# Gate and up lines with one matmul of 512 columns for both halves of the activation

## The chip, the cores and the metric

The kernel runs on one core of a Trainium2 chip. The metric is the device time of one execution in microseconds (us). Before the change it is 1159.81 us, the median of 3 runs (1159.59 to 1160.43).

## The reference

The program computes two blocks on 256 tokens (272 with 16 meta tokens) of 1024 features. The first block has two layers with two kinds of attention. The second block has a feed-forward stage, a mixer (gated linear attention and sparse attention), a second feed-forward stage and an embedding stage. The change concerns the two feed-forward stages, called ffn0 and ffn1 in the kernel:

```python
def swiglu(x, w_in, w_out):                      # w_in 1024 x 5632, w_out 2816 x 1024
    gate, up = jnp.split(x @ w_in, 2, axis=-1)
    return (jax.nn.silu(gate) * up) @ w_out

h = h + 0.5 * swiglu(rms_norm_2(h, ffn1_norm[i]), ffn1_w_in[i], ffn1_w_out[i])
h = h + hybrid_mixer(...)
h = h + 0.5 * swiglu(rms_norm_2(h, ffn2_norm[i]), ffn2_w_in[i], ffn2_w_out[i])
```

All is float32. The factor of the norm is the same for all features of a token, so the kernel multiplies by it after the matmuls (`scale`).

## The kernel before

Features lie on the 128 partitions and tokens along the free dimension. A float32 value is split in two parts of the shorter type float32r: a rounded high half (`_hi`) and the rest (`_lo`). A product of two such values is summed from three matmuls: high weight by high activation, high weight by low activation, low weight by high activation.

**Lines and units.** A "line" is 128 output features of one projection: 8 k-tiles of 128 inputs ("down" in the feed-forward stages: 11), three matmuls each, all into one bank of PSUM. A "unit" holds the weights of two lines (16 blocks of 128 x 128, 1 MB). Of the feed-forward stages, unit j for j = 0 to 21 is gate line j and up line j, and 16 units of 11 blocks follow for the two halves of each of 8 down lines.

**Where the weights come from.** SP loads unit u into one of three slots of `raw` (`load_unit`, L726) once the low halves of unit u-3 have been made. ACT rounds the unit to `w_hi` in two instructions (`cut_to`, L866; L875 and L876), once PE has finished the lines of unit u-3. DVE subtracts, `w_lo = raw - w_hi`, in four pieces of 512 columns (L1343; four of 384, 384, 384 and 256 in a down unit). For some lines elsewhere POOL does this; never in a feed-forward stage. `lo_after` (L1348) fixes in which place of DVE's program the pieces come: behind gate line j the last two pieces of unit j+1, behind up line j the first two of unit j+2. PE waits for the pieces that a line needs before its first matmul.

**A turn of a feed-forward stage.** Each engine has one queue and works in the order of its program. All five programs are written out by hand; the sequence for each j is this.

- PE: gate line j, then up line j (`line`, L2128; its matmuls have line 2147). The lines use four banks in turn (`line0`, `line1`, `result0`, `result1`), and a line waits until the line four places before has been read out.
- DVE: gate line j times `scale` into `prod` (L1415), `act_lo` of j-1 (L1758), two pieces of w_lo, in ffn0 for j = 2 to 9 one `first_result` (L1739), up line j times `scale` into `prod2` (L1415), two pieces of w_lo, and the two instructions of `finish` (L1750: (tanh + 1) times gate; L1753: times up). Turn 1 of ffn0 also has the two instructions of `last_norm`.
- ACT: the two `w_hi` instructions of unit j+2, tanh of gate line j (L1112), `act_hi` of j-1 (L1103).

`act_lo` of j-1 waits for `act_hi` of j-1, and ACT makes that only after tanh of j, which waits for gate line j.

Ahead of ffn0 and ffn1 the factor of the norm is computed by PE, ACT and DVE in turn (`root_of`, `rstd_of`); meanwhile PE already runs the first lines. Behind the turns come 16 half down lines; DVE adds each to `h`.

Of the kernel before, what the change touches and what calls it, by code (L numbers as in the profile page):

```python
# [54 lines left out]
SH = 8  # L55
# [435 lines left out]
class Alloc:  # L491
# [11 lines left out]
    def sem(self, name):  # L503
        return self.stack.enter_context(self.nc.semaphore(name))
# [5 lines left out]
def hybrid_blocks_kernel(nc, weights, tokens, embeds, small_in, small2_in, rpb, consts_in, consts2_in, levels_in,  # L510
# [7 lines left out]
    w_lo = sb("w_lo", [CUT, UB * P], F32R)  # L518

    h = sb("h", [KT, TOK])  # L520
    x_hi = sb("x_hi", [KT, TOK], F32R)
    x_lo = sb("x_lo", [KT, TOK], F32R)
    y_hi = sb("y_hi", [KT, TOK], F32R)
    y_lo = sb("y_lo", [KT, TOK], F32R)
    wide = sb("wide", [KT, TOK])
    scale = sb("scale", [TOK])
    root = sb("root", [2, TOK])
# [88 lines left out]
    od_hi_ready, od_ready = sem("od_hi_ready"), sem("od_ready")  # L616
    p_hi_ready, p_ready, pp_ready = sem("p_hi_ready"), sem("p_ready"), sem("pp_ready")
    pg_raw, pg_used = sem("pg_raw"), sem("pg_used")
    means_ready = sem("means_ready")
    gate_ready = sem("gate_ready")  # L620
    stored = sem("stored")
    hg_ready, last_root, out_pool = sem("hg_ready"), sem("last_root"), sem("out_pool")

    first, second = (x_hi, x_lo), (y_hi, y_lo)
    x_of = dict(layer0=first, mixed0=first, layer1=second, mixed1=second, ffn0=first, mixer=first, mixed2=first,
                ffn1=second, embed=first)
    y_of = dict(layer0=second, layer1=first)
# [44 lines left out]
    mean_p = a2.sb("mean_p", [P])  # L672
    levels = a2.sb("levels", [len(HALVES) + 1, P], U32)
    p_in = turned[:, :, 0:SEQ]
    p_hi = a2.sb("p_hi", [2, SEQ], F32R)
    p_lo = a2.sb("p_lo", [2, SEQ], F32R)
    pp = wide[:, :, 0:SEQ]
    a3 = Alloc(nc)
    act_hi = a3.sb("act_hi", [FT, SEQ], F32R)
    act_lo = a3.sb("act_lo", [FT, SEQ], F32R)  # L680
    a3.close()
    a3 = Alloc(nc)
    gg_hi, gg_lo = y_hi[:, :, 0:SEQ], y_lo[:, :, 0:SEQ]
    low = turned[:, 0, 0:SEQ]
    index_k = a3.sb("index_k", [SEQ])
    index_q = a3.sb("index_q", [PAIRS, SEQ])
# [16 lines left out]
    a4 = Alloc(nc)  # L703
    dq = wide[:, :, 0:SEQ]
    mgate = {n: a4.sb(f"mgate_{n}", [KT, SEQ]) for n in "gs"}
    od_hi = a4.sb("od_hi", [SH, SEQ], F32R)
    od_lo = a4.sb("od_lo", [SH, SEQ], F32R)

    rbias = a4.sb("rbias", [RING, SEQ])
    score = root[:, :, 0:SEQ]  # L710
# [151 lines left out]
    def _(act):  # L862
# [235 lines left out]
        def ffn(f):  # L1098
            name = f"ffn{f}"

            def round_act(j):
                act.wait_ge(act_full, FT * f + j + 1)
                act.activation(act_hi[:, j], prod2[:, j % 2, 0:SEQ], ACT.Copy).then_inc(act_hi_ready, 1)  # L1103

            for j in range(FT):
                cut_to(UNIT[(name, "gate", j)] + CUT - 1)
                n = FT * f + j
                act.wait_ge(act_raw, n + 1)

                if j >= 2:  # L1110
                    act.wait_ge(act_half, n - 1)
                act.activation(th[:, j % 2, 0:SEQ], prod[:, j % 2, 0:SEQ], ACT.Tanh, scale=0.5).then_inc(act_tanh, 1)  # L1112
                if j:
                    round_act(j - 1)
            round_act(FT - 1)
# [162 lines left out]
        cut_to(STAGES["ffn1"] + CUT - 1)  # L1278
        root_of(("ffn1", "norm"), SEQ)
        act.wait_ge(embeds_in, 16)  # L1280
        act.activation(p_hi[:, :, :], p_in, ACT.Copy).then_inc(p_hi_ready, 1)
        ffn(1)


# [34 lines left out]
    def _(dve):  # L1319
# [423 lines left out]
        def ffn(f):  # L1743
            name = f"ffn{f}"

            def finish(j):

                n = FT * f + j
                dve.wait_ge(act_tanh, n + 1)
                dve.scalar_tensor_tensor(prod[:, j % 2, 0:SEQ], th[:, j % 2, 0:SEQ], 1.0, prod[:, j % 2, 0:SEQ],  # L1750
                                         ALU.add, ALU.mult).then_inc(act_half, 1)
                dve.wait_ge(act_half, n + 1)
                dve.tensor_tensor(prod2[:, j % 2, 0:SEQ], prod[:, j % 2, 0:SEQ], prod2[:, j % 2, 0:SEQ],  # L1753
                                  ALU.mult).then_inc(act_full, 1)

            def rest_of_act(j):
                dve.wait_ge(act_hi_ready, FT * f + j + 1)
                dve.tensor_tensor(act_lo[:, j], prod2[:, j % 2, 0:SEQ], act_hi[:, j].bitcast(F32),  # L1758
                                  ALU.subtract).then_inc(act_ready, 1)

            for j in range(FT):
                scaled_line((name, "gate", j), prod[:, j % 2, 0:SEQ]).then_inc(act_raw, 1)
                if j:
                    rest_of_act(j - 1)
                lo_after(name, "gate", j)
                if f == 0 and j == 1:
                    last_norm()
                if f == 0 and 2 <= j < KT + 2:
                    first_result(j - 2)
                scaled_line((name, "up", j), prod2[:, j % 2, 0:SEQ]).then_inc(act_up, 1)  # L1770
                lo_after(name, "up", j)
                dve.wait_ge(act_up, FT * f + j + 1)
                finish(j)
            rest_of_act(FT - 1)
            for m in range(KT):

                dve.scalar_tensor_tensor(h[:, m, 0:SEQ], line_wait((name, "down", m, 0))[:, 0:SEQ], 0.25,
                                         h[:, m, 0:SEQ], ALU.mult, ALU.add).then_inc(down_used, 1)
                lo_after(name, "down", m, 0)
                if m:  # L1780
                    rest_of_h(("mixer", "embed")[f], m - 1, SEQ)
                dve.wait_ge(down_used, KT * f + m + 1)
                dve.scalar_tensor_tensor(h[:, m, 0:SEQ], line_wait((name, "down", m, 1))[:, 0:SEQ], 0.25,
                                         h[:, m, 0:SEQ], ALU.mult, ALU.add).then_inc(h_ready, 1)
                if m < KT - 1:
                    lo_after(name, "down", m, 1)
            one_piece()
            dve.wait_ge(h_ready, H_BATCH[name] + KT)
            rest_of_h(("mixer", "embed")[f], KT - 1, SEQ)
            lo_after(name, "down", KT - 1, 1)  # L1790
# [289 lines left out]
        lo_after("mixer", "mix", KT - 1)  # L2080
        rstd_of(("ffn1", "norm"), SEQ, scale[:, 0:SEQ])
        dve.wait_ge(p_hi_ready, 1)
        dve.tensor_tensor(p_lo[:, :, :], p_in, p_hi[:, :, :].bitcast(F32), ALU.subtract).then_inc(p_ready, 1)
        ffn(1)


# [28 lines left out]
    def _(pe):  # L2115
# [15 lines left out]
        def line(key, n, src=None, depth=KT, first=0, at=None, ready=None, last=None):  # L2131


            if at is None:
                at = key[-1] % 2 * KT
            hi, lo = unit(key)
            src_hi, src_lo = src or x_of[key[0]]
            bank = line_open(key)
            for k in range(depth):
                if last and k == depth - 1:  # L2140
                    last()
                if ready:
# [252 lines left out]
        def ffn(f):  # L2395
            name = f"ffn{f}"
            for j in range(FT):
                if j == 0:
                    line((name, "gate", j), SEQ, at=0, ready=x_tile(name), last=(lambda: norm_sum(name, SEQ)) if f else None)
                else:  # L2400
                    line((name, "gate", j), SEQ, at=0)
                line((name, "up", j), SEQ, at=KT)
                if (f, j) == (0, 0):

                    two_norm_sums()
            for m in range(KT):
                for half in range(2):
                    first = half * FT // 2
                    line((name, "down", m, half), SEQ, (act_hi, act_lo), FT // 2, first, 0,
                         ready=(lambda k: pe.wait_ge(act_ready, FT * f + first + k + 1)) if m == 0 else None)  # L2410

        ffn(0)
# [38 lines left out]
        def line_by_token(key):  # L2451
# [1 line left out]

            t = key[2] % TILES
            hi, lo = (w.rearrange("p (m k) c -> p k m c", m=2) for w in unit(key))
            src_hi, src_lo = (x[:, :, t * P:(t + 1) * P] for x in x_of[key[0]])
            bank = line_open(key)[:, 0:2 * P].rearrange("p (m c) -> p m c", c=P)
            for k in range(KT):
                for m, (stay, move) in enumerate([(src_hi, hi), (src_hi, lo), (src_lo, hi)]):
# [103 lines left out]
        for i in range(len(DSA_JOBS) + 2):  # L2563
            if i < len(DSA_JOBS):
# [1 line left out]
                if i == KT:  # L2566
                    pe.wait_ge(gg_ready, KT)
                name, m = DSA_FILLERS[i]
                line(("mixer", name, m), SEQ, (gg_hi, gg_lo) if name == "yg" else None)
            if 1 <= i <= len(DSA_JOBS):  # L2570
                dsa_turn(i - 1)
            if i >= 2:
                dsa_values(i - 2)
        for m in range(KT):
            line(("mixer", "ys", m), SEQ, (od_hi, od_lo),
                 ready=(lambda k: pe.wait_ge(od_ready, k + 1)) if m == 0 else None)
        for m in range(KT):
            line(("mixer", "mix", m), SEQ, x_of["mixed2"], ready=x_tile("mixed2") if m == 0 else None)
# [1 line left out]
        ffn(1)  # L2580
        pe.wait_ge(p_ready, 1)
        for m in range(KT):
            line(("embed", "pp", m), SEQ, (p_hi, p_lo), 2, 0, 2 * m)
        for m in range(KT):
            if m == 0:
                line(("embed", "pg", m), SEQ, ready=x_tile("embed"), last=lambda: norm_sum("embed", SEQ))
# [157 lines left out]
```

## Time and profile before

| | |
|---|---|
| median of 3 runs | 1159.81 us |
| span of the profiled execution | 1158.5 us |
| PE busy | 1118.8 us (97%) |
| DVE busy | 826.3 us (71%) |
| ACT busy | 628.0 us (54%) |
| POOL busy | 256.3 us (22%) |
| chain that ended last | PE 79%, DVE 13%, ACT 4% |
| granted clock of PE over the span | 0.9 to 1.0 of full in each of 40 slices |

The page and the views come from one profiled execution. Its own time is not listed beside the runs; its span, from the first to the last instruction on the engines, is 1158.5 us, and the median of the runs lies 1.3 us above it. Matmuls are pipelined: the profile gives one of 256 columns 0.28 us, but in a full stream the next starts 0.12 us later. So the time of a stretch of matmuls is read from their starts, and busy time on PE means only that the stream did not stop. Instructions of DVE and ACT overlap by 0.08 us in the same way where the second does not wait for the first.

### The profile page before, as it was taken

To read this page: it belongs to the slowest core of one execution; us is meant where nothing else is said; L and a number is where in the kernel's file an instruction comes from. 1 tells how busy PE (TensorE), PEld (TensorE's weight loads), DVE (VectorE), ACT (ScalarE), POOL (GpSimd) and SP (SyncE) were. 2 spreads that over 40 slices of the span, in tenths; PEclk is the share of its full clock that TensorE was granted. 3 is DMA by queue.
4 is the path that set the end of the run, shared out by engine and by line. 5 is a ranking of instruction groups with operands and counts; after the bars stand their busy time and mean duration, and the time that the engine had idled before them with its cause. 6 is when DMAs were issued, how large, how long until landed. Compare 5 with 4: busy or idle time off the path is not lost.

```text
span 1158.5 us, 23093 instructions
## 1 busy us (share of the span) xinstructions
PE 1118.8 (97%) x9108; PEld 1096.5 (95%) x9108; DVE 826.3 (71%) x1843; ACT 628.0 (54%) x1164; POOL 256.3 (22%) x214
## 2 busy tenths in 40 slices
PE   6999999999999999999999999989999999999996
PEld 6999999999999999999999999978999999999995
DVE  7964356879544687888766799577857877777666
ACT  6555545564655547544444653584455654444464
POOL 1056553200656614000000008300770000000000
PEclk9999999999999999999999999999999999999998
DMA  6454333354433434555455453225453555544551
GB/s 244 154 182 146 110 120 105 128 178 154 184 132 124 154 116 167 216 189 184 163 194 190 180 203 127 110 76 173 175 168 139 191 182 182 182 171 176 180 203 37
DMA packets 38635, 185.05 MB, mean 160 GB/s; under 512 B 12536, under 2 KB 14840, under 8 KB 19968
## 3 DMA queue, kind: packets, MB, share of 16 engines
q1 hardware_dynamic: 38528, 183.57, 45.2%
q8 instruction: 73, 1.20, 0.4%
q14 instruction: 34, 0.28, 0.1%
HBM read 182.49 MB, written 1.06 MB: 158 GB/s over the span
## 4 chain that ended last, share of the span: by engine, by line
PE 79%; DVE 13%; ACT 4%; issue 2%; DMA 1%; DVEq 0%; POOL 0%; SPq 0%; ACTq 0%
PE line L2147 49%; PE result L2147 18%; DVE w_lo L1343 4%; PE line L2460 2%; PE turn L2304 1%; PE result L2338 1%; PE score L2281 1%; PE score L2479 1%; PE stat L2338 1%; PE score L2285 1%; ACT w_hi L876 1%; ACT w_hi L875 1%; DVE root L1378 1%; DVE rstd L1365 1%; PE score L2147 1%
## 5 line engine op out<-in xcount | busy, mean ns | idle before, releaser
L852 POOL TENSOR_TENSOR w_lo<-raw,w_hi 128x512 fp32r<-128x512 f32 x168 | 224.2, 1366 | 545.7 <-ACT w_hi L875 545.6
L1343 DVE TENSOR_TENSOR w_lo<-raw,w_hi 128x512 fp32r<-128x512 f32 (+2 forms) x544 | 338.2, 666 | 3.0 <-ACT w_hi L910 2.0
L2147 PE MATMUL line<-x_hi,w_hi 128*128 128x256 f32 (+1 forms) x1048 | 309.1, 295 | 16.0 <-DVE x_lo L1399 9.3
L2147 PE MATMUL line<-x_hi,w_lo 128*128 128x256 f32 (+1 forms) x1048 | 299.1, 285 | 0.0
L2147 PE MATMUL line<-x_lo,w_hi 128*128 128x256 f32 (+1 forms) x1048 | 298.8, 285 | 0.0
L875 ACT ACTIVATE w_hi<-raw 128x1024 fp32r<-128x1024 f32 (+1 forms) x177 | 179.5, 1014 | 91.1 <-PE line L2147 36.5
L2147 PEld LDWEIGHTS line<-x_hi,w_hi 128*128 128x128 f32 x1048 | 199.4, 190 | 22.7 <-issue 13.5
L2147 PEld LDWEIGHTS line<-x_lo,w_hi 128*128 128x128 f32 x1048 | 199.1, 190 | 0.9
L2147 PEld LDWEIGHTS line<-x_hi,w_lo 128*128 128x128 f32 x1048 | 199.6, 190 | 0.0
L2147 PE MATMUL line<-y_hi,w_hi 128*128 128x256 f32 (+1 forms) x656 | 192.6, 294 | 1.0 <-DVE y_lo L1407 0.3
L2147 PE MATMUL line<-y_hi,w_lo 128*128 128x256 f32 (+1 forms) x656 | 185.4, 283 | 0.0
L2147 PE MATMUL line<-y_lo,w_hi 128*128 128x256 f32 (+1 forms) x656 | 185.2, 282 | 0.0
L876 ACT ACTIVATE w_hi<-raw 128x1024 fp32r<-128x1024 f32 (+1 forms) x178 | 175.6, 987 | 0.0
L2147 PEld LDWEIGHTS line<-y_hi,w_hi 128*128 128x128 f32 x656 | 123.8, 189 | 2.9 <-DVE w_lo L1343 0.9
L2147 PEld LDWEIGHTS line<-y_lo,w_hi 128*128 128x128 f32 x656 | 123.5, 188 | 0.8
L2147 PEld LDWEIGHTS line<-y_hi,w_lo 128*128 128x128 f32 x656 | 124.0, 189 | 0.0
L2147 PE MATMUL result<-x_hi,w_hi 128*128 128x256 f32 (+1 forms) x232 | 65.8, 283 | 0.1
L2147 PE MATMUL result<-x_lo,w_hi 128*128 128x256 f32 (+1 forms) x232 | 65.4, 282 | 0.0
L2147 PE MATMUL result<-x_hi,w_lo 128*128 128x256 f32 (+1 forms) x232 | 65.4, 282 | 0.0
L858 POOL TENSOR_TENSOR wide<-hg,rstd 128x512 f32<-128x512 f32 x1 | 1.7, 1702 | 285.2 <-DVE rstd L1365 285.2
L1017 ACT ACTIVATE probs<-score,top 128x272 f32<-128x272 f32 (+2 forms) x66 | 29.6, 449 | 57.4 <-DVE top L1563 35.4
L2147 PE MATMUL result<-y_lo,w_hi 128*128 128x256 f32 x192 | 54.1, 282 | 0.0
(376 smaller groups left out, 2354.0 us busy)
## 6 DMA issues: line engine op xcount, KB each, us to landing
raw<-in_weights SPq DMA_DIRECT2D x145, 1024.0 KB, 4.8
raw<-in_weights SPq DMA_DIRECT2D x32, 704.0 KB, 4.1
rel_raw<-in_rpb SPq DMA_DIRECT2D x64, 24.0 KB, 4.8
h<-in_tokens SPq DMA_DIRECT2D x2, 544.0 KB, 6.4
raw<-in_weights SPq DMA_DIRECT2D x2, 512.0 KB, 6.3
rbias<-bias_by_distance SPq DMA_DIRECT2D x8, 128.0 KB, 4.9
out<-wide SPq DMA_DIRECT2D x4, 256.0 KB, 2.5
consts<-in_consts SPq DMA_DIRECT2D x1, 960.0 KB, 7.1
```

What stands on the lines that cost most here:

```text
L852: pool.tensor_tensor(w_lo[:, u % CUT, at], raw[:, u % RAW, at], w_hi[:, u % CUT, at].bitcast(F32), ALU.subtract).then_inc(lo_pool, 1)
L875: act.activation(w_hi[:, v % CUT, 0:half], raw[:, v % RAW, 0:half], ACT.Copy).then_inc(hi_cut, 1)
L876: act.activation(w_hi[:, v % CUT, half:n], raw[:, v % RAW, half:n], ACT.Copy).then_inc(hi_cut, 1)
L1017: act.activation(probs[0:m, place % 2, first:first + keys], score_bank[s % 2][0:m, 0:keys], ACT.Exp, bias=top[0:m, n % 2, 0:1], scale=-1.0 ...
L1343: dve.tensor_tensor(w_lo[:, u % CUT, at], raw[:, u % RAW, at], w_hi[:, u % CUT, at].bitcast(F32), ALU.subtract).then_inc(lo_cut, 1)
L1365: ins = dve.scalar_tensor_tensor(r if out_ is None else out_, v, -3.0, r, ALU.add, ALU.mult)
L1378: dve.scalar_tensor_tensor(v, stat_at(key)[:, 0:n], EPS, v, ALU.add, ALU.mult).then_inc(stat_read, 1)
L2147: ins = pe.matmul(bank[:, 0:n], stay, move[:, first + k, 0:n], start=(k, m) == (0, 0), stop=(k, m) == (depth - 1, 2))
L2281: ins = pe.matmul(s[:, 0:TOK], qa[:, c, t * P:(t + 1) * P], ka_half[:, half * TOK:(half + 1) * TOK], start=True, stop=True)
L2285: ins = pe.matmul(s[:, 0:KEYS_B], qb[:, c, t * P:(t + 1) * P], kb[:, c, t, half], start=True, stop=True)
L2338: ins = pe.matmul(single_bank[pair % 2][:, cols], tn[:, b * P:(b + 1) * P], v[:, kt, cols], start=(half, b) == (0, 0), stop=b == both)
L2460: ins = pe.matmul(bank, stay[:, k], move[:, k], start=(k, m) == (0, 0), stop=(k, m) == (KT - 1, 2))
```

## The change

In gate and up lines the two matmuls that share the high half of a weight become one. It moves both halves of the activation past it, 512 columns in two separate runs of 256, and fills the bank: columns 0 to 255 get high by high, columns 256 to 511 high by low. The third matmul (low weight by high activation) adds to columns 0 to 255 as before. To make the two halves reachable by one operand they now lie in one buffer (`x`, `y`, and for the sake of one helper also `act`, `p`, `od`).

The two column ranges must now be added. ACT copies the upper one to SBUF (`low_sum`), DVE adds the lower one (`both_sums`), waits for its own result and multiplies by `scale`. There is one place for each copy (gate, up), so a copy waits until the copy before has been used.

```diff
+TWO_SUMS = {_g for _g in LINES if _g[1] in ("gate", "up")}
...
-    x_hi = sb("x_hi", [KT, TOK], F32R)
-    x_lo = sb("x_lo", [KT, TOK], F32R)
+    x = sb("x", [2, KT, TOK], F32R)
...
+    low_sums, sums_of_line = wide[:, 0:2, 0:SEQ], wide[:, 2:4, 0:SEQ]
...
# ACT
+            def low_sum(kind, j):
+
+                at = int(kind == "up")
+                bank = line_wait((name, kind, j))
+                if FT * f + j:
+                    act.wait_ge((act_raw, act_up)[at], FT * f + j)
+                act.activation(low_sums[:, at], bank[:, SEQ:2 * SEQ], ACT.Copy).then_inc(low_sum_out, 1)
+
             for j in range(FT):
-                cut_to(UNIT[(name, "gate", j)] + CUT - 1)
+                low_sum("gate", j)
                 n = FT * f + j
                 act.wait_ge(act_raw, n + 1)
...
                 act.activation(th[:, j % 2, 0:SEQ], prod[:, j % 2, 0:SEQ], ACT.Tanh, scale=0.5).then_inc(act_tanh, 1)
+                low_sum("up", j)
                 if j:
                     round_act(j - 1)
...
# DVE
+            def both_sums(kind, j, dst):
+                at = int(kind == "up")
+                bank = line_wait((name, kind, j))
+                dve.wait_ge(low_sum_out, 2 * (FT * f + j) + at + 1)
+                link(dve.tensor_tensor(sums_of_line[:, at], bank[:, 0:SEQ], low_sums[:, at], ALU.add))
+                return dve.tensor_tensor(dst, sums_of_line[:, at], scale[:, 0:SEQ], ALU.mult)
...
-                scaled_line((name, "gate", j), prod[:, j % 2, 0:SEQ]).then_inc(act_raw, 1)
+                both_sums("gate", j, prod[:, j % 2, 0:SEQ]).then_inc(act_raw, 1)
...
-                scaled_line((name, "up", j), prod2[:, j % 2, 0:SEQ]).then_inc(act_up, 1)
+                both_sums("up", j, prod2[:, j % 2, 0:SEQ]).then_inc(act_up, 1)
...
# PE
+                if key in TWO_SUMS:
+
+                    pe.matmul(bank[:, 0:2 * n].rearrange("p (h t) -> p h t", h=2), hi[:, at + k], both[:, :, first + k, 0:n],
+                              start=k == 0, stop=False)
+                    ins = pe.matmul(bank[:, 0:n], lo[:, at + k], src_hi[:, first + k, 0:n], start=False,
+                                    stop=k == depth - 1)
+                    continue
```

(`line_wait` on ACT begins with `cut_to`, so the `w_hi` instructions keep their place.)

DVE in a turn of ffn1 before the change (`prod` is both `prod` and `prod2`), from the gate line to the next:

```order
L1415 TENSOR_TENSOR prod<-line,scale 128x256 [waits line_done]
L1758 TENSOR_TENSOR act_lo<-prod,act_hi 128x256 [waits act_hi_ready]
L1343 TENSOR_TENSOR w_lo<-raw,w_hi 128x512 [waits hi_cut] x2
L1415 TENSOR_TENSOR prod<-line,scale 128x256 [waits line_done]
L1343 TENSOR_TENSOR w_lo<-raw,w_hi 128x512 [waits hi_cut] x2
L1750 SCALAR_TENSOR_TENSOR prod<-th,prod 128x256 [waits act_tanh,act_up]
L1753 TENSOR_TENSOR prod<-prod 128x256 [waits act_half]
L1415 TENSOR_TENSOR prod<-result,scale 128x256 [waits line_done]
```

The same turn on DVE after the change (`wide` holds the copied and the added sums, `act` is both halves of the activation):

```order
L1769 TENSOR_TENSOR wide<-line,wide 128x256 [waits low_sum_out,line_done]
L1770 TENSOR_TENSOR prod<-wide,scale 128x256 [waits dve_step]
L1784 TENSOR_TENSOR act<-prod,act 128x256 [waits act_hi_ready]
L1362 TENSOR_TENSOR w_lo<-raw,w_hi 128x512 [waits hi_cut] x2
L1769 TENSOR_TENSOR wide<-line,wide 128x256 [waits low_sum_out,line_done]
L1770 TENSOR_TENSOR prod<-wide,scale 128x256 [waits dve_step]
L1362 TENSOR_TENSOR w_lo<-raw,w_hi 128x512 [waits hi_cut] x2
L1776 SCALAR_TENSOR_TENSOR prod<-th,prod 128x256 [waits act_tanh,act_up]
L1779 TENSOR_TENSOR prod<-prod 128x256 [waits act_half]
```

Each scaled line has become two instructions, the first with a wait for ACT and the second with a wait for the first; nothing else has moved.

ACT in the same place before the change, from tanh to tanh:

```order
L1112 ACTIVATE th<-prod 128x256 [waits act_raw]
L1103 ACTIVATE act_hi<-prod 128x256 [waits act_full]
L875 ACTIVATE w_hi<-raw 128x1024 [waits line_done,raw_in1]
L876 ACTIVATE w_hi<-raw 128x1024
L1112 ACTIVATE th<-prod 128x256 [waits act_half,act_raw]
```

And after the change:

```order
L1130 ACTIVATE th<-prod 128x256 [waits act_raw]
L1121 ACTIVATE wide<-line 128x256 [waits act_up,line_done]
L1113 ACTIVATE act<-prod 128x256 [waits act_full]
L885 ACTIVATE w_hi<-raw 128x1024 [waits line_done,raw_in1]
L886 ACTIVATE w_hi<-raw 128x1024
L1121 ACTIVATE wide<-result 128x256 [waits act_raw,line_done]
L1130 ACTIVATE th<-prod 128x256 [waits act_half,act_raw]
```

The copy of the up line stands between tanh and the rounded activation of the turn before; the copy of the next gate line stands behind the two `w_hi` instructions.

## Rows read from the trace of the kernel before

**Rows 1.** The page: its first line, and the engines' busy time.
```profile
span 1158.5 us, 23093 instructions
PE 1118.8 (97%) x9108; PEld 1096.5 (95%) x9108; DVE 826.3 (71%) x1843; ACT 628.0 (54%) x1164; POOL 256.3 (22%) x214
```

**Rows 2.** Chain of waits, whole span: start us, us, engine and line, matmuls.
```profile
126.17 3.02 PE line L2147 x24
...
577.40 5.68 PE result L2147 x48
...
678.33 5.66 PE line L2460 x48
...
1053.61 7.80 PE result L2147 x66
```

**Rows 3.** Chain of waits, 440 to 482 us.
```profile
476.39 1.30 DVE w_lo L1343 x2
...
477.74 3.11 PE result L2147 x24
```

**Rows 4.** Timeline of DVE in ffn0: start us, us, instruction, idle before.
```profile
502.25 0.42 DVE L1415 TENSOR_TENSOR prod<-result,scale 128x256 f32<-128x256 f32 x1
503.46 0.43 DVE L1758 TENSOR_TENSOR act_lo<-prod,act_hi 128x256 fp32r<-128x256 f32 x1 [0.79 <-ACT act_hi L1103]
503.80 1.29 DVE L1343 TENSOR_TENSOR w_lo<-raw,w_hi 128x512 fp32r<-128x512 f32 x2
505.00 0.48 DVE L1739 SCALAR_TENSOR_TENSOR h<-h,small,rstd 128x256 f32<-128x256 f32 x1
505.40 0.41 DVE L1415 TENSOR_TENSOR prod<-result,scale 128x256 f32<-128x256 f32 x1
505.73 1.28 DVE L1343 TENSOR_TENSOR w_lo<-raw,w_hi 128x512 fp32r<-128x512 f32 x2
506.94 0.42 DVE L1750 SCALAR_TENSOR_TENSOR prod<-th,prod 128x256 f32<-128x256 f32 x1
507.39 0.43 DVE L1753 TENSOR_TENSOR prod<-prod 128x256 f32<-128x256 f32 x1
507.73 0.42 DVE L1415 TENSOR_TENSOR prod<-line,scale 128x256 f32<-128x256 f32 x1
```

**Rows 5.** Timeline of ACT in the same turn.
```profile
502.70 0.42 ACT L1112 ACTIVATE th<-prod 128x256 f32<-128x256 f32 x1 [1.70 <-DVE prod L1415]
503.02 0.40 ACT L1103 ACTIVATE act_hi<-prod 128x256 fp32r<-128x256 f32 x1
504.52 1.06 ACT L875 ACTIVATE w_hi<-raw 128x1024 fp32r<-128x1024 f32 x1 [1.10 <-DMA raw<-in_weights]
```

**Rows 6.** Timeline of DVE at the first and behind the last turn of ffn1.
```profile
933.65 0.69 DVE L2083 TENSOR_TENSOR p_lo<-turned,p_hi 128x512 fp32r<-128x512 f32 x1
934.26 0.42 DVE L1415 TENSOR_TENSOR prod<-result,scale 128x256 f32<-128x256 f32 x1
...
1050.85 0.42 DVE L1415 TENSOR_TENSOR prod<-line,scale 128x256 f32<-128x256 f32 x1
...
1058.12 1.83 DVE L1343 TENSOR_TENSOR w_lo<-raw,w_hi 128x384 fp32r<-128x384 f32 x4
```

**Rows 7.** Timeline of DVE in the first two turns of ffn0.
```profile
465.80 0.76 DVE L1415 TENSOR_TENSOR prod<-line,scale 128x256 f32<-128x256 f32 x2
...
468.46 0.42 DVE L1415 TENSOR_TENSOR prod<-result,scale 128x256 f32<-128x256 f32 x1
...
470.05 0.43 DVE L1758 TENSOR_TENSOR act_lo<-prod,act_hi 128x256 fp32r<-128x256 f32 x1 [1.17 <-ACT act_hi L1103]
...
474.84 0.42 DVE L1415 TENSOR_TENSOR prod<-line,scale 128x256 f32<-128x256 f32 x1
```

**Rows 8.** Timeline of ACT there: the load of the table for tanh.
```profile
465.79 1.28 ACT L1112 ACT_TABLE_LOAD   x1
```

**Rows 9.** Stretches: busy us and count of each engine, PE clock, DMA, GB/s.
```profile
765.00:780.00 15.00, 10.38 (x81) 9.82 (x80) 11.39 (x27) 12.70 (x24) 0.00 (x0) 0.96 0.20 71
...
815.00:830.00 15.00, 13.53 (x111) 13.14 (x110) 14.11 (x45) 6.08 (x11) 10.10 (x8) 1.00 0.57 211
```

More of the change, by code:

```diff
@@ L618, in hybrid_blocks_kernel @@
     pg_raw, pg_used = sem("pg_raw"), sem("pg_used")
+    low_sum_out = sem("low_sum_out")
     means_ready = sem("means_ready")
@@ L622, in hybrid_blocks_kernel, with halves @@
     hg_ready, last_root, out_pool = sem("hg_ready"), sem("last_root"), sem("out_pool")
-    first, second = (x_hi, x_lo), (y_hi, y_lo)
+    def halves(both):
+        return both[:, 0], both[:, 1], both
+    first, second = halves(x), halves(y)
     x_of = dict(layer0=first, mixed0=first, layer1=second, mixed1=second, ffn0=first, mixer=first, mixed2=first,
@@ L674, in hybrid_blocks_kernel @@
     p_in = turned[:, :, 0:SEQ]
-    p_hi = a2.sb("p_hi", [2, SEQ], F32R)
-    p_lo = a2.sb("p_lo", [2, SEQ], F32R)
+    p = a2.sb("p", [2, 2, SEQ], F32R)
+    p_hi, p_lo = p[:, 0], p[:, 1]
+    low_sums, sums_of_line = wide[:, 0:2, 0:SEQ], wide[:, 2:4, 0:SEQ]
     pp = wide[:, :, 0:SEQ]
     a3 = Alloc(nc)
-    act_hi = a3.sb("act_hi", [FT, SEQ], F32R)
-    act_lo = a3.sb("act_lo", [FT, SEQ], F32R)
+    act_both = a3.sb("act", [2, FT, SEQ], F32R)
+    act_hi, act_lo = act_both[:, 0], act_both[:, 1]
     a3.close()
     a3 = Alloc(nc)
-    gg_hi, gg_lo = y_hi[:, :, 0:SEQ], y_lo[:, :, 0:SEQ]
+    gg = y[:, :, :, 0:SEQ]
+    gg_hi, gg_lo = gg[:, 0], gg[:, 1]
     low = turned[:, 0, 0:SEQ]
@@ L705, in hybrid_blocks_kernel @@
     mgate = {n: a4.sb(f"mgate_{n}", [KT, SEQ]) for n in "gs"}
-    od_hi = a4.sb("od_hi", [SH, SEQ], F32R)
-    od_lo = a4.sb("od_lo", [SH, SEQ], F32R)
+    od = a4.sb("od", [2, SH, SEQ], F32R)
+    od_hi, od_lo = od[:, 0], od[:, 1]
     rbias = a4.sb("rbias", [RING, SEQ])
@@ L1280, in _ @@
         act.wait_ge(embeds_in, 16)
-        act.activation(p_hi[:, :, :], p_in, ACT.Copy).then_inc(p_hi_ready, 1)
+        act.activation(p_hi, p_in, ACT.Copy).then_inc(p_hi_ready, 1)
         ffn(1)
@@ L2082, in _ @@
         dve.wait_ge(p_hi_ready, 1)
-        dve.tensor_tensor(p_lo[:, :, :], p_in, p_hi[:, :, :].bitcast(F32), ALU.subtract).then_inc(p_ready, 1)
+        dve.tensor_tensor(p_lo, p_in, p_hi.bitcast(F32), ALU.subtract).then_inc(p_ready, 1)
         ffn(1)
@@ L2136, in line @@
             hi, lo = unit(key)
-            src_hi, src_lo = src or x_of[key[0]]
+            src_hi, src_lo, both = src or x_of[key[0]]
             bank = line_open(key)
@@ L2408, in ffn @@
                     first = half * FT // 2
-                    line((name, "down", m, half), SEQ, (act_hi, act_lo), FT // 2, first, 0,
+                    line((name, "down", m, half), SEQ, halves(act_both), FT // 2, first, 0,
                          ready=(lambda k: pe.wait_ge(act_ready, FT * f + first + k + 1)) if m == 0 else None)
@@ L2455, in line_by_token @@
             hi, lo = (w.rearrange("p (m k) c -> p k m c", m=2) for w in unit(key))
-            src_hi, src_lo = (x[:, :, t * P:(t + 1) * P] for x in x_of[key[0]])
+            src_hi, src_lo = (x[:, :, t * P:(t + 1) * P] for x in x_of[key[0]][:2])
             bank = line_open(key)[:, 0:2 * P].rearrange("p (m c) -> p m c", c=P)
@@ L2568, in _ @@
                 name, m = DSA_FILLERS[i]
-                line(("mixer", name, m), SEQ, (gg_hi, gg_lo) if name == "yg" else None)
+                line(("mixer", name, m), SEQ, halves(gg) if name == "yg" else None)
             if 1 <= i <= len(DSA_JOBS):
@@ L2574, in _ @@
         for m in range(KT):
-            line(("mixer", "ys", m), SEQ, (od_hi, od_lo),
+            line(("mixer", "ys", m), SEQ, halves(od),
                  ready=(lambda k: pe.wait_ge(od_ready, k + 1)) if m == 0 else None)
@@ L2582, in _ @@
         for m in range(KT):
-            line(("embed", "pp", m), SEQ, (p_hi, p_lo), 2, 0, 2 * m)
+            line(("embed", "pp", m), SEQ, halves(p), 2, 0, 2 * m)
         for m in range(KT):
```

3 lines of the change are left out of this document (1 added, 2 removed).

## The prediction

> **What bounds the kernel now.** I read the page first. PE is busy for 1118.8 of 1158.5 us, DVE for 826.3 [rows 1], so at first sight TensorE sets the time and anything that shortens its stream pays. I then followed the chain of waits through the two feed-forward stages (FFN 0, from 461 us; FFN 1, from 931 us), since only their gate and up lines change. In the steady part the chain is PE alone: a turn j (gate line j and up line j, 48 matmuls) takes 5.68 us, 118.3 ns from one matmul to the next; the last turn of FFN 0 ends at 583.08, the last of FFN 1 at 1053.61 [rows 2]. At the start of FFN 0 the same chain shows something else: up line 3 starts at 477.74, 0.05 us after DVE's w_lo pieces for it end at 477.69 [rows 3]. There DVE was the later one. So I read DVE instruction by instruction in a turn where it is behind.
>
> Call G(j) the start of DVE's first instruction on gate line j. From G = 502.25 to the next, 507.73, is 5.48 us [rows 4]. The steps between starts are: gate scaled, then idle until ACT's act_hi, 1.21; act_lo 0.34; two w_lo pieces 1.20; first_result 0.40; up scaled 0.33; two w_lo pieces 1.21; the two halves of `finish` 0.45 and 0.34. Nowhere in it does DVE wait for PE. The idle 0.79 us is a round trip: gate scaled, ACT's tanh 0.45 later, act_hi 0.32 behind it, act_lo 0.44 behind that [rows 4, 5]. The round thus takes 5.48 with first_result (eight turns, j = 2 to 9 of FFN 0) and 5.08 without. PE needs 5.68. The cover is 0.6 us a turn, and 0.2 in those eight: TensorE and the DVE-ACT round are nearly level.
>
> **The change, part by part.**
>
> *TensorE.* For each of 8 k-tiles of 88 lines, two matmuls of 256 columns become one of 512. No line of the trace streams 512 columns past such a weight. Nearest rows: 256 columns take 118.3 ns start to start, 272 take 3.02/24 = 125.8 [rows 2]. At 2.4 GHz (the granted level) 256 columns stream in 107 ns, so each matmul has some 11.6 ns on top, and merging two saves that once. Bounds: 213 ns (512 columns with nothing on top) and 237 (two present ones, nothing saved). I take 225. A line then takes 8 x (225 + 118.3) = 2.75 us instead of 2.84, a turn 5.49. If TensorE alone set the time, 88 x 8 x 11.6 ns = 8.2 us would go. That the 512 columns come from two places I cost at nothing: the L2460 matmuls move two separate runs of 128 columns and take 5.66/48 = 118 ns [rows 2].
>
> The Trainium skill, "TensorE: Matmul & The Clock Gate", section "Back-to-back issue gap", gives about 131 ns a matmul at 512 columns as sustained in a stream with weight loads. By it a line would take 2.0 us and TensorE would be freed of some 70 us. The 256-column rows at 118 ns, which follow the column count, do not fit so small a step, and no row here has 512 columns; the sum below doesn't use it.
>
> *DVE.* Each scaled line (one instruction out of PSUM, with `scale`) becomes an addition and then a multiplication that waits for it. The nearest dependent pair is `finish`, 0.45 from start to start (506.94 to 507.39), the nearest independent step 0.33 to 0.34 [rows 4]. I take 0.45 for each added instruction, so 0.90 a turn. Bounds 0.33 and 0.48 each, the latter a first_result whole.
>
> *ACT.* A copy of 256 columns is like act_hi: 0.32 a step, 0.40 alone [rows 5]. What matters is where it stands. The copy for up line j stands ahead of act_hi(j-1), and DVE waits for act_hi(j-1) before it writes act_lo, the w_lo pieces of unit j+1 and all behind them; those pieces are what PE's up line j+1 waits for. So the up copy adds 0.32 to the round (bounds 0.30 and 0.42). At the start of a stage, where DVE isn't behind, it even has to wait for PE's up line itself. The gate copy adds nothing while DVE is behind: gate line j+1 is done and ACT through its w_hi pieces about 1.8 us before G(j+1). The weight transfers stay covered too: w_hi waits 1.1 us for one at 504.52 [rows 5], and the slot for the next is given free by the w_lo pieces, one round earlier, with the round now longer.
>
> New round: 5.08 + 0.90 + 0.32 = **6.30 us**, and 6.70 with first_result. It is longer than TensorE's 5.49, so DVE and ACT set every turn. What PE does in 5.49 hides behind it, the saving included; PE waits some 0.8 us a turn, at the up line, for w_lo. The round leaves room for a 512-column matmul of up to 6.30/16 - 118 = 276 ns.
>
> *The sum, FFN 1.* G(0) is 934.26 and stays: the first gate copy fits in while DVE makes p_lo [rows 6]. Turn 0 has no act_lo: 0.45 + 0.34 + 1.24 + 0.45 + 0.34 + 1.20 + 0.45 + 0.34 = 4.8, so G(1) = 939.1. 20 rounds of 6.30, and 0.5 for turn 20, which cuts four pieces of 384 columns instead of two of 512, give G(21) = 1065.6. From G(21) to the end of the w_lo pieces of the third "down" unit is 1050.85 to 1059.95 = 9.1 us now [rows 6] and 1.2 more after: 1075.9. TensorE, which started that unit at 1061.41 (1053.61 + 7.80 [rows 2]), then waits for it: **+14.5 us**. After that "down" gives nothing back: its pace is PE's.
>
> *FFN 0.* Here DVE is the later one from the start. Turn 0: the first gate copy delays the sum by 0.4; the up copy stands behind ACT's 1.28 us table load and the tanh, so the up addition starts near 468.25, and G(1) moves from 468.46 to about 471.0. Turn 1 adds 1.2 less the 0.4 which it already waits for ACT (468.46 to 470.05 is 1.59, not 1.21) [rows 7, 8]. G(2) = 474.84 + 3.4 = 478.2. 8 x 6.70 + 11 x 6.30 + 0.5 = 123.4 gives G(21) = 601.6; 10.3 more is 611.9, against 583.08 + 7.80 = 590.88: **+21.0 us**.
>
> At both stage starts the norm matmul comes 0.1 us earlier: -0.2 together. Sum 35.3 us on a span of 1158.5, so 1193.8. The median of the runs, 1159.81, lies 1.3 above the profiled span, which I add: 1195.1. All else in the diff (halves of one buffer instead of two buffers) issues the same instructions.
>
> **Rivals.**
> - *The forecast:* the DVE-ACT round sets the turn, about 1195 us. For it: a round already at 5.48 with no wait for PE in it. Chance 0.82.
> - *TensorE still sets the turn (faster).* The round would have to stay below 5.49: the 1.22 us would have to fit into 0.4. That could be if the additions fell into DVE's idle 0.79 and 0.42 and the act_hi copy didn't wait for the up copy. Against it: both stand in order in one queue, and the idle is itself part of the round. Price: -8.2 + 1159.8 = 1152. Decides from a round of 5.49 down. Chance 0.04.
> - *Half hidden.* The two added instructions cost 0.33 each and the up copy nothing: round 5.74, so 42 rounds x 0.06 over PE's present 5.68, with 3.2 for the eight first_result turns and about 3 at starts and ends: 1169. Chance 0.05.
> - *The clock falls.* PE would pause for 13% of the time. In 765:780, with PE busy for 10.38 of 15 us, the granted clock fell to 0.96 from 1.00; in 815:830, at 13.53 of 15, it stayed at 1.00 [rows 9]. The expected pauses are like the latter. If a tenth of the gate and up turns (27 us at the new pace) ran at 1.2 GHz, their 4.3 turns of 11 us would cost some 20 us more: 1215. Chance 0.05. The Trainium skill, same page, section "A second HAM failure mode: psum-queue depth-cycling", says that short idles between groups at 512 columns made the clock go back and forth in another kernel; the 815:830 row speaks against it at this share of idle.
> - *The wide matmul costs over 276 ns.* At 300 a line takes 3.35 us, a turn 6.70: 1211. No row excludes it; the two-run matmuls of L2460 make it unlikely. Chance 0.04.
>
> **How the numbers follow.** A measurement of this kernel tells 0.2% (2.3 us) from no change. Slower by more than that: forecast, half hidden, clock and wide matmul, 0.95, less 0.01 for what no case names: 0.94. Faster: 0.04. Same: 0.02. The bounds of the added prices move the round from 6.30 to 6.04 (0.33, 0.33, 0.30) or 6.46 (0.48, 0.48, 0.42): 42 rounds, -11 or +7 us, so 1184 to 1202 for the forecast alone. The clock and wide cases pull the upper end to 1209; the half hidden and the faster case stay outside.
>
> **What would show it.** DVE rounds of 6.30 (6.70 for j = 2 to 9 of FFN 0) at even spacing; act_lo starting about 1.98 after G(j) with ACT in the order tanh, copy, act_hi ahead of it; a PE wait near 0.8 us for w_lo at each up line and none at the "down" lines beyond the first few; the first act_lo wait in each stage longest; a 512-column matmul 225 ns from the next. It would be wrong if DVE waited for PE in mid-stage, if the act_hi copy came before the up copy's wait mattered, or if the PE clock row fell below 10 in these slices.

## The result, and the profile after

The changed kernel takes 1198.1 us (median of 4 runs, 1197.8 to 1198.17) against 1159.7 (4 runs) for the kernel before. The ratio is 1.0333, with a 95% interval of 1.032 to 1.0345: slower, by 38 us. The forecast was 1195, within 1184 to 1209.

The page of the kernel after: its first line, the engines' busy time, and PE's and DVE's rows of 40 slices of the span.

```profile
span 1196.1 us, 22033 instructions
PE 1129.7 (94%) x8404; PEld 1065.4 (89%) x8404; DVE 858.7 (72%) x1931; ACT 651.0 (54%) x1252; POOL 256.2 (21%) x214
...
PE   6999999999999998889999999989999999998996
...
DVE  7954456879336687888866799677757788887666
```

PE has 704 matmuls fewer and is nevertheless busy for longer than in [rows 1]: that number counts a running stream, not work. What tells is its share, 94% after 97%, and the 8s in its row that the row before lacks: three slices in ffn0 (448 to 538 us) and one at the down units of ffn1 (1076 to 1106 us). The chain of waits has moved from PE to DVE. Page part 4 of the kernel after, share of the span by engine:

```profile
PE 58%; DVE 27%; ACT 7%; issue 6%; DMA 2%; DVEq 0%; POOL 0%; ACTq 0%; SPq 0%
```

Before, PE had 79% and DVE 13%. This is DVE's timeline for a turn of ffn0 in the kernel after (columns as in [rows 4], which it answers to):

```profile
504.96 0.41 DVE L1769 TENSOR_TENSOR wide<-line,wide 128x256 f32<-128x256 f32 x1
505.41 0.42 DVE L1770 TENSOR_TENSOR prod<-wide,scale 128x256 f32<-128x256 f32 x1
506.90 0.42 DVE L1784 TENSOR_TENSOR act<-prod,act 128x256 fp32r<-128x256 f32 x1 [1.06 <-ACT act L1113]
507.24 1.29 DVE L1362 TENSOR_TENSOR w_lo<-raw,w_hi 128x512 fp32r<-128x512 f32 x2
508.44 0.48 DVE L1758 SCALAR_TENSOR_TENSOR h<-h,small,rstd 128x256 f32<-128x256 f32 x1
508.84 0.41 DVE L1769 TENSOR_TENSOR wide<-line,wide 128x256 f32<-128x256 f32 x1
509.29 0.42 DVE L1770 TENSOR_TENSOR prod<-wide,scale 128x256 f32<-128x256 f32 x1
509.63 1.28 DVE L1362 TENSOR_TENSOR w_lo<-raw,w_hi 128x512 fp32r<-128x512 f32 x2
510.83 0.41 DVE L1776 SCALAR_TENSOR_TENSOR prod<-th,prod 128x256 f32<-128x256 f32 x1
511.28 0.42 DVE L1779 TENSOR_TENSOR prod<-prod 128x256 f32<-128x256 f32 x1
511.63 0.42 DVE L1769 TENSOR_TENSOR wide<-result,wide 128x256 f32<-128x256 f32 x1
```

From 504.96 to 511.63 is 6.67 us (forecast 6.70, before 5.48). Each addition costs 0.45 (504.96 to 505.41, 508.84 to 509.29), and the idle before act_lo has grown from 0.79 to 1.06. ACT's timeline in the same turn shows by what, and answers to [rows 5]:

```profile
505.87 0.42 ACT L1130 ACTIVATE th<-prod 128x256 f32<-128x256 f32 x1 [2.52 <-DVE prod L1770]
506.19 0.37 ACT L1121 ACTIVATE wide<-line 128x256 f32<-128x256 f32 x1
506.46 0.41 ACT L1113 ACTIVATE act<-prod 128x256 fp32r<-128x256 f32 x1
```

The up line's copy stands between tanh and act_hi for 0.27 us (506.19 to 506.46). ACT waits 2.52 us ahead of tanh and does not limit anything by its amount of work. PE pays: its timeline at an up line of ffn1.

```profile
1002.43 0.28 PE L2174 MATMUL result<-y,w_lo 128*128 128x256 f32 x1
1002.55 0.39 PE L2172 MATMUL result<-y,w_hi 128*128 128x512 f32 x1
1002.78 0.28 PE L2174 MATMUL result<-y,w_lo 128*128 128x256 f32 x1
1003.50 0.51 PE L2172 MATMUL result<-y,w_hi 128*128 128x512 f32 x1 [0.43 <-DVE w_lo L1362]
```

The next matmul starts 0.72 us after the last, not 0.12: 0.60 us lost, to w_lo. The idle of 0.43 in brackets is less, since it counts only from the modelled end of the matmul before. Wide to narrow is 0.23 us here, narrow to wide 0.12. The first wide matmul behind the pause takes 0.34 (1003.50 to 1003.84), 0.11 more, and both together are the 0.7 us by which a turn is longer than TensorE's own.

### The profile page after: what moved, and what is told of

Same layout as the page of the kernel before. It is cut to its first block, busy times and chain, and to the rows that moved or that the text cites. A ratio compares the mean times of both kernels' runs of the same rounds, so it can differ in the third digit from the quotient of the medians.

```text
span 1196.1 us, 22033 instructions
## 1 busy us (share of the span) xinstructions
PE 1129.7 (94%) x8404; PEld 1065.4 (89%) x8404; DVE 858.7 (72%) x1931; ACT 651.0 (54%) x1252; POOL 256.2 (21%) x214
## 3 DMA queue, kind: packets, MB, share of 16 engines
HBM read 182.49 MB, written 1.06 MB: 153 GB/s over the span
## 4 chain that ended last, share of the span: by engine, by line
PE 58%; DVE 27%; ACT 7%; issue 6%; DMA 2%; DVEq 0%; POOL 0%; ACTq 0%; SPq 0%
PE line L2180 37%; DVE w_lo L1362 12%; PE result L2180 7%; DVE wide L1769 2%; PE line L2493 2%; DMA raw<-in_weights 2%; DVE prod L1770 2%; ACT wide L1121 1%; PE turn L2337 1%; DVE prod L1776 1%; ACT act L1113 1%; PE result L2371 1%; PE score L2314 1%; PE score L2512 1%; PE stat L2371 1%
## 5 line engine op out<-in xcount | busy, mean ns | idle before, releaser
L2180 PE MATMUL line<-x,w_hi 128*128 128x256 f32 (+1 forms) x1744 | 336.5, 293 | 14.2 <-DVE x L1418 9.3
L2180 PEld LDWEIGHTS line<-x,w_hi 128*128 128x128 f32 x1744 | 276.4, 191 | 21.6 <-issue 13.6
L2180 PE MATMUL line<-x,w_lo 128*128 128x256 f32 (+1 forms) x872 | 250.3, 287 | 0.0
L2180 PE MATMUL line<-y,w_hi 128*128 128x256 f32 (+1 forms) x960 | 183.3, 291 | 1.0 <-DVE prod L1688 0.3
L2180 PEld LDWEIGHTS line<-x,w_lo 128*128 128x128 f32 x872 | 166.9, 191 | 0.0
L2180 PEld LDWEIGHTS line<-y,w_hi 128*128 128x128 f32 x960 | 150.2, 188 | 3.7 <-DVE w_lo L1362 0.9
L2180 PE MATMUL line<-y,w_lo 128*128 128x256 f32 (+1 forms) x480 | 135.9, 283 | 0.0
L2180 PEld LDWEIGHTS line<-y,w_lo 128*128 128x128 f32 x480 | 90.6, 189 | 0.0
L2172 PE MATMUL result<-x,w_hi 128*128 128x512 f32 x176 | 63.7, 400 | 6.6 <-DVE w_lo L1362 6.6
L2180 PE MATMUL result<-act,w_hi 128*128 128x256 f32 x352 | 64.5, 285 | 2.4 <-DVE w_lo L1362 2.4
```

Source lines behind the costliest of these rows:

```text
L2172: pe.matmul(bank[:, 0:2 * n].rearrange("p (h t) -> p h t", h=2), hi[:, at + k], both[:, :, first + k, 0:n], start=k == 0, stop=False)
```

## The experiments

Each kernel was timed beside the kernel before. The runs of one kernel spread by 1 to 5 us; the last section shows from what. Medians and ratios are given, and where it matters the lowest run.

**The wide matmuls alone.** The changed kernel, with its sums left out (so the high-by-low products of gate and up lines are missing from its result):

```diff
 # ACT
-                low_sum("gate", j)
+                cut_to(UNIT[(name, "gate", j)] + CUT - 1)
...
-                low_sum("up", j)
 # DVE, and the same for "up"
-                both_sums("gate", j, prod[:, j % 2, 0:SEQ]).then_inc(act_raw, 1)
+                scaled_line((name, "gate", j), prod[:, j % 2, 0:SEQ]).then_inc(act_raw, 1)
```

> The 512-column matmuls stay, but the sums are not added: DVE scales columns 0 to 255 alone, in one instruction, and ACT copies nothing (the high-by-low products of gate and up lines are left out of the result). The theory (the round of DVE and ACT sets the turn) expects the turn to fall back to TensorE's own. With the pair of matmuls at 0.349 us start to start, as the changed kernel's unstalled stretches show, against 3 x 0.118 = 0.355, 704 pairs give 4 us: 1155.5 (1154 to 1158). My prediction's price for the wide matmul (225 ns) would give 1151.5. The rival that the wide matmuls themselves, or the way they fill a bank, make the kernel slower expects 1175 or more.

Measured: 1157.2 us, ratio 0.9978 (0.9969 to 0.9988). That is near the upper end of the 1154 to 1158 expected. All of the loss is gone, so it is not in the matmuls. The chain of waits of this kernel in ffn1 (start us, us, what) is PE alone and shows the pace:

```profile
955.49 0.23 PE line L2171
...
977.84 0.24 PE line L2171
...
1000.18 0.24 PE line L2171
```

From 955.49, the first matmul of a line, to 1000.18 are eight turns, and 44.7/8 = 5.59 us is a turn, 0.349 us a pair. Three matmuls of 256 columns took 0.355 [rows 2]. The gain is 704 x 0.006 = 4 us in theory and 2.3 to 2.5 us by the measurement (the kernel before, timed with it, took 1159.5).

**The sums alone.** TensorE does three matmuls of 256 columns again, but one of them fills the upper half of the bank; ACT and DVE do all of the changed kernel's work:

```diff
-                    pe.matmul(bank[:, 0:2 * n].rearrange("p (h t) -> p h t", h=2), hi[:, at + k], both[:, :, first + k, 0:n],
-                              start=k == 0, stop=False)
+                    pe.matmul(bank[:, 0:n], hi[:, at + k], src_hi[:, first + k, 0:n], start=k == 0, stop=False)
+                    pe.matmul(bank[:, n:2 * n], hi[:, at + k], src_lo[:, first + k, 0:n], start=False,
+                              stop=False)
```

> TensorE goes back to three matmuls of 256 columns for each k-tile, the high-by-low one into columns 256 to 511 of the bank; the copies on ACT and the additions on DVE stay as in the changed kernel. The theory expects no difference from the changed kernel: 1198 (1195 to 1201), DVE rounds of 6.28 us and PE waiting 0.6 us a turn instead of 0.7. The rival that the wide matmul is to blame expects 1160 to 1175.

Measured: 1196.8 us, ratio 1.0323 (1.0304 to 1.0341), as the changed kernel. DVE's rounds in ffn1 are 6.28 us, its idle before act_lo 1.06. PE waits for w_lo 15 times from 478 to 575 us, 8.9 us or 0.59 a time; in the changed kernel 16 times from 478 to 583, 10.8 us or 0.68 a time. Together with the first experiment this shows that the whole loss comes with the sums, and that while they set the turn TensorE's saving is worth nothing.

**The copy out of the round.** Two calls change places on ACT:

```diff
-                low_sum("up", j)
                 if j:
                     round_act(j - 1)
+                low_sum("up", j)
```

> The changed kernel with two ACT calls in the other order: the rounded activation of the turn before comes ahead of the up line's copy. The theory takes the copy out of the round: 0.26 us less a round (the copy's step in the trace, 472.31 to 472.57), rounds of 6.02, at least 42 x 0.26 = 11 us less: 1187 (1185 to 1189). The rival that only the amount of work on DVE matters, and ACT's order doesn't, expects 1198.

Measured: 1185.3 us, ratio 1.0224 (1.0208 to 1.024), 12.8 us less than the changed kernel at the same work. DVE's timeline in ffn1, a round of 6.01 us:

```profile
1020.83 0.42 DVE L1769 TENSOR_TENSOR wide<-result,wide 128x256 f32<-128x256 f32 x1
1021.28 0.42 DVE L1770 TENSOR_TENSOR prod<-wide,scale 128x256 f32<-128x256 f32 x1
1022.50 0.43 DVE L1784 TENSOR_TENSOR act<-prod,act 128x256 fp32r<-128x256 f32 x1 [0.79 <-ACT act L1113]
...
1026.84 0.42 DVE L1769 TENSOR_TENSOR wide<-line,wide 128x256 f32<-128x256 f32 x1
```

The idle is back at 0.79. That ACT's order counts, and not only DVE's amount of work, is shown. The two traces show where most of the 12.8 us are. From the last lines ahead of ffn0 to its third down unit this kernel takes 170.5 us (434.40 to 604.87) and the changed kernel 176.2 (435.42 to 611.57); from the last lines ahead of ffn1 it is 162.6 against 168.1. That is 11.2 us in the rounds, as estimated. Another 1.0 lies ahead of ffn0 (434.40 against 435.42), where the two kernels do the same work, and is spread, not the move.

**The additions out of the round.** ACT copies and DVE waits for the copy, but does not add (the high-by-low products are missing from the result again):

```diff
-                link(dve.tensor_tensor(sums_of_line[:, at], bank[:, 0:SEQ], low_sums[:, at], ALU.add))
-                return dve.tensor_tensor(dst, sums_of_line[:, at], scale[:, 0:SEQ], ALU.mult)
+                return dve.tensor_tensor(dst, bank[:, 0:SEQ], scale[:, 0:SEQ], ALU.mult)
```

> The changed kernel with ACT's copies, in their places, and with DVE waiting for them, but without the two additions a turn (the high-by-low products are left out of the result). The theory: the round is 5.08 + 0.26 = 5.34 us, below TensorE's 5.58, so in mid-stage TensorE sets the turn and only the ends of the stages lose (the up copy makes DVE wait for PE, 2 to 4 us in all): 1160 (1157 to 1163). The rival that the wait for ACT's copy is what costs, whatever DVE computes, expects 1175 or more.

Measured: 1163.2 us, ratio 1.0033 (1.002 to 1.0046), 0.2 above the upper end of what I expected. 35 of the 38 us come with the additions. In mid-stage PE sets the turn: gate lines follow each other on DVE at 1003.97 and 1009.56, 5.59 apart, with idle 1.29 before act_lo. What is left, against the wide matmuls alone, are waits of PE for w_lo at the stage's ends: 2.0, 0.8 and 0.4 us in the first turns of ffn0 and 1.2 behind the last turn of each stage.

**The same work, in another order.** On DVE act_lo goes behind the two w_lo pieces, and the trip over ACT passes while DVE makes them:

```diff
-                if j:
-                    rest_of_act(j - 1)
                 lo_after(name, "gate", j)
+                if j:
+                    rest_of_act(j - 1)
```

> The changed kernel with act_lo of the turn before behind DVE's two w_lo pieces, not ahead of them. DVE does the same instructions, but the round trip over ACT (tanh, up copy, act_hi; idle 1.06 us a turn) now passes while DVE makes w_lo. The theory expects rounds of 5.2 us of DVE work, under TensorE's 5.58, so TensorE sets the turn again: 1156 (1154 to 1160), PE without waits in mid-stage. The rival that the work itself is too much (0.9 us a turn more on DVE) expects at least 1175; the rival that the wide matmuls are to blame expects 1190 or more.

Measured: 1161.0 us, ratio 1.0012 (1.0003 to 1.0021), 1 us above the upper end of what I expected (1156, within 1154 to 1160). Moving one instruction a turn gives back 37 of the 38 us, with both additions and both copies still done. DVE in ffn1, one turn of 5.59 us:

```profile
980.51 0.42 DVE L1769 TENSOR_TENSOR wide<-result,wide 128x256 f32<-128x256 f32 x1
980.96 0.43 DVE L1770 TENSOR_TENSOR prod<-wide,scale 128x256 f32<-128x256 f32 x1
981.30 1.29 DVE L1362 TENSOR_TENSOR w_lo<-raw,w_hi 128x512 fp32r<-128x512 f32 x2
982.96 0.43 DVE L1784 TENSOR_TENSOR act<-prod,act 128x256 fp32r<-128x256 f32 x1 [0.37 <-ACT act L1113]
...
986.10 0.42 DVE L1769 TENSOR_TENSOR wide<-line,wide 128x256 f32<-128x256 f32 x1
```

The idle is 0.37 now, and it is PE's doing: ACT's up copy (982.23) has waited 0.40 us for PE's up line. By the stretches view PE is busy for all of 980 to 1040 us, DVE for 54.8 of the 60, 91%. An engine may be that full and cost nothing if no one waits for it. The one long wait of PE in this kernel is at the start of ffn0, where the kernel before waits 0.8 us at most (timeline of PE):

```profile
469.54 0.57 PE L2172 MATMUL line<-x,w_hi 128*128 128x512 f32 x1 [2.47 <-DVE w_lo L1362]
```

Behind this wait the mean granted clock is 0.57 of full until 473.5 us, so most of that stretch runs at 1.2 GHz. Two short waits of 0.24 us stand at the third down unit of each stage.

**That, with three moves on ACT.**

```diff
             for j in range(FT):
                 low_sum("gate", j)
+                if j == 0:
+                    low_sum("up", j)
...
-                low_sum("up", j)
                 if j:
                     round_act(j - 1)
+                    low_sum("up", j)
+            cut_to(UNIT[(name, "down", 0, 0)] + CUT - 1)
             round_act(FT - 1)
```

> The kernel with act_lo behind the w_lo pieces, and three more moves on ACT: act_hi of the turn before comes ahead of the up line's copy; in turn 0 the up copy comes ahead of tanh and its table load; the w_hi instructions of the third down unit come ahead of the last act_hi. The theory says that what that kernel still loses is the 2.5 us wait at the second up line of ffn0 and one of about 1.6 us at the third down unit of each stage, with a fall of the clock behind it. It expects these gone or below 1 us, and 1157 (1155 to 1159), as with the wide matmuls alone. The rival that the added work costs something all along (DVE and ACT reading banks beside TensorE) expects 1160 or 1161 as before the moves.

Measured: 1159.3 us, ratio 0.999 (0.998 to 0.9999), just above the 1157 (1155 to 1159) that I expected and below the rival's 1160 or 1161: the median doesn't decide between them. The wait at the start fell from 2.47 to 1.28. The one that I expected at the third down unit wasn't there to remove: the kernel without these moves waits 0.24 us at that place in ffn0, not 1.6. The twelve runs lie in two groups, five at 1155.4 to 1156.7 and seven at 1159.3 to 1160.4; the lower one is as low as the wide matmuls alone (lowest 1155.4). None of the upper group was profiled. The profiled run, of the lower group, shows no standing cost of the added work: from 930 to 1048 us, in ffn1, it has 678 matmuls, as many as the kernel with the wide matmuls alone has from 932 to 1050, with PE busy throughout and the clock at 1.00 in both. This is the best complete version tried, and it is as fast as the kernel before within what a measurement tells (2.3 us).

**The kernel before with act_lo moved.** The diff is the one above, made in the kernel before.

> The kernel before with one move: act_lo of the turn before behind the two w_lo pieces. The theory: only the first turns of ffn0 gain, where PE waited 0.8 and 0.2 us for w_lo behind DVE's idle 0.79; elsewhere the round is hidden already. 1158.5 (1157.5 to 1159.5), a ratio of 0.999 to the kernel before. The rival, that the round costs PE time in every turn of the kernel before too, expects 1150 or less.

Measured: 1159.8 us, ratio 0.9998 (0.9989 to 1.0006): no difference, and 0.3 us above the 1157.5 to 1159.5 that I expected. PE's waits of 0.8 and 0.2 us at the start of ffn0 are gone from the trace, but 1 us can't be told from none by the medians. The rival, that the round cost PE time in every turn of the kernel before, falls.

**The halves side by side.** The wide matmuls alone, with the second run of columns nearer (`y` is changed in the same way):

```diff
-    x = sb("x", [2, KT, TOK], F32R)
+    x = sb("x", [KT, 2, TOK], F32R)[:, :, :, :].rearrange("p k h t -> p h k t")
```

> As the kernel with the wide matmuls alone (the high-by-low products of gate and up lines are again left out of the result), but the two halves of an activation tile lie side by side (the second run starts 272 columns behind the first, not 2176). The open point is why a wide matmul takes 0.23 us and not 0.225. If the jump between the two runs costs it, the pair falls from 0.349 to about 0.343 us and the time by 4 us, to 1153. If the distance doesn't matter (my theory: the L2460 matmuls already move two far runs at the normal pace), the pair stays at 0.349 and the time at 1157 (1155 to 1159).

Measured: 1156.7 us, ratio 0.9974 (0.9964 to 0.9984), as with the halves far apart. The chain in ffn1 goes from 933.09 to 944.29 in two turns (32 pairs), 0.350 us a pair. The distance is not what a wide matmul pays for; why it takes 0.23 us stays open.

## Why the prediction was right, step by step

**The mechanism** was right: the round over DVE and ACT sets the turn, and what showed it before the change was the one place where DVE was behind, the first turns of ffn0 [rows 3, 4]. The sums-alone, copy-first and act_lo runs each move the time as a round would, and the first of them is untouched by what TensorE does.

**The terms**, forecast and found:

| | forecast | measured |
|---|---|---|
| added instruction on DVE | 0.45 | 0.45 |
| up copy in the round | 0.32 | 0.27 |
| TensorE's own turn | 5.49 | 5.59 |
| PE's loss a turn | 0.8 | 0.7 |
| round, and with first_result | 6.30, 6.70 | 6.28, 6.67 |
| G(1), G(2) of ffn0 | 471.0, 478.2 | 471.07, 478.27 |
| G(21) of ffn0 | 601.6 | 601.22 |
| third down unit of ffn0 starts | 611.9 | 611.57 |
| ffn1, up to its third down unit | +14.5 | +14.1 |
| 512-column matmul | 0.225 | 0.23 |

The price of the copy was taken from act_hi's step. In the kernel after, the copies step a little faster: 0.26 to 0.27 us to the next instruction, against 0.30 to 0.31 for act_hi. The copy reads PSUM and act_hi reads SBUF and writes the rounded type; which of the two makes the difference was not tested. The wide matmul saves half of what I gave it, 6 ns a pair and not 11.6, so TensorE alone would have won 4 us, not 8.2. In the changed kernel this had no effect on the time, and PE loses 0.7 us a turn instead of 0.8. One sign did not come: the first idle before act_lo is no longer than the others, 1.06 us at 473.01 and at 964.15 as everywhere. The chances of the four slower cases add up to 0.96, not 0.95; nothing hangs on that.

By the rate that the Trainium skill gives ("TensorE: Matmul & The Clock Gate", "Back-to-back issue gap", 131 ns a matmul sustained at 512 columns), a pair would take some 0.25 us, an estimate from that figure and the 118 ns of [rows 2]. The trace has 0.35. The measurement decides: this kernel's operands do not reach that rate.

**The 3 us that were missing** (1195 forecast, 1198 found). In the span 2.3 are missing, 37.6 found for 35.3, and most of that is the clock, which I had as a rival only for whole turns at 1.2 GHz. These are rows of the chain of waits, first of the kernel after, then of the kernel before:

```profile
611.57 9.59 PE result L2180 x66
...
679.83 4.56 PE line L2180 x24
...
702.28 5.66 PE line L2493 x48
...
803.55 3.10 PE line L2180 x24
...
930.54 20.86 PE line L2180 x174
...
1098.63 8.07 PE line L2180 x66
```

```profile
657.38 3.04 PE line L2147 x24
...
779.09 4.53 PE line L2147 x24
...
907.38 20.85 PE line L2147 x174
```

The 66 matmuls from 611.57 take 9.59 us; they take 7.80 in a stream without a stop [rows 2] and 8.07 behind the same wait at full clock (1098.63). That is 1.8 us, of which 1.5 are the clock and 0.3 the start behind the wait. The 24 from 679.83 take 4.56 instead of 3.04 in the same line before, another 1.5. At 803.55 the fall that the kernel before has at 779.09 is missing, which gives 0.8 back on balance (the shift goes from 702.28 - 678.33 = 23.95 to 930.54 - 907.38 = 23.16). The sum then closes: 20.7 (third down unit of ffn0, 611.57 - 590.88) + 1.8 + 1.5 - 0.8 + 14.1 + 0.3 (8.07 for 7.80) = 37.6, which is 1196.1 - 1158.5. So the clock added 2.2 us and the starts behind two waits 0.6, while the rounds came out 0.5 shorter than forecast (34.8 for 35.3). The other 0.7 us of the 3 is the step from span to run time: I added 1.3, and the median of the changed kernel lies 2.0 above its profiled span.

**The rivals.** "TensorE still sets the turn" needed a round below 5.49. It was false for the order of the change and became true by moving act_lo, since DVE then works in what was idle time; that was the rival's condition. "Half hidden" was wrong: every added instruction cost its full 0.45. The wide matmul takes 230 ns, far from 276. The clock stayed at 1.00 in mid-stage, in spite of PE's pause in each turn: in the kernel after, the stretches 500 to 560 and 960 to 1060 us have PE busy for 53.8 of 60 and 93.6 of 100 us and a granted clock of 1.00. I read this from the stretches, since 9 is the highest digit in the page's row for the clock, before as after; its last slice is an 8 in both pages, so the table ahead of the prediction is too high there (0.87 over the last 29 us before). The Trainium skill, "TensorE: Matmul & The Clock Gate", section "A second HAM failure mode: psum-queue depth-cycling", tells of another kernel, with bf16 matmuls of 512 columns, in which short idles between groups made the clock go back and forth. These stretches do not show that for pauses of 0.6 us in turns of 6.3.

## What to carry to other kernels

Where two engines hand work back and forth, write down the round in starts to starts, from a stretch in which the engine concerned is behind, and compare it with the bounding engine's turn: the difference is the whole cover, however idle that engine looks on average. What is added inside the round costs in full once the cover is gone; what is done while the round trip is waited for cost next to nothing here (37 of 38 us came back), so look for an independent piece of work to put there before taking work away. A saving on the bounding engine that needs work on the round trip of its suppliers should be counted only down to the length of that round.

## What the runs showed of the hardware that was not expected

A wait of the same length can end with a fall of the clock or without one. In the kernel after, PE waits for w_lo at the third down unit of each stage, with 2.02 us of idle in both cases. The stretches behind the two waits (columns as in [rows 9]):

```profile
611.57:613.50 1.93, 1.93 (x11) 1.93 (x12) 1.93 (x5) 1.68 (x5) 0.00 (x0) 0.68 0.47 117
613.50:615.50 2.00, 2.00 (x12) 2.00 (x11) 0.09 (x1) 0.56 (x1) 0.00 (x0) 0.50 0.94 324
...
1098.63:1100.60 1.97, 1.97 (x16) 1.97 (x17) 1.97 (x5) 1.72 (x5) 0.00 (x0) 1.00 0.43 126
1100.60:1102.60 2.00, 2.00 (x19) 2.00 (x18) 0.05 (x1) 0.53 (x1) 0.00 (x0) 1.00 0.91 299
```

After the first the granted clock is 0.50 of full, 1.2 GHz, and 12 matmuls start in 2 us where 19 do after the second. In the kernel with the sums alone both waits end in a fall (9.60 us for 66 matmuls twice), in the copy-first kernel neither does (8.07 twice). At the start of ffn0 it is the same: behind PE's wait of 2.47 us in the kernel with act_lo moved the mean granted clock was 0.57 for 4 us, behind one of 2.00 in the kernel without the additions it stayed at 1.00. What decides between the two ends stays open.

The fall at 611.57 costs 1.5 us (9.59 for 8.07). The clock also goes with much of the spread between the runs of one kernel: in the best version the runs at 1155.4 to 1156.7 us have a mean granted clock of 0.995, those at 1159.3 to 1160.4 have 0.991 to 0.993; of the 48 runs of the kernel before beside the experiments, those with 0.997 took 1157.5 to 1158.2 us and those with 0.992 or 0.993 took 1159.6 to 1162.7. A change worth 1 to 2 us can't be seen by medians under such a spread, but can in the traces, as the waits of PE which it removes.
